# One decoder step in fp32: the order of items, dense groups and outputs in the attention ticks

## The reference

```
h  = RMSNorm(x) * (1 + a1) + s1                       # a1, s1, ... = silu(c) @ w_ada + b_ada
[q | k | v | hc | B | C | ga | gb] = h @ w_in
A-branch: stick-breaking attention, 8 heads x 64, strictly causal
          A[t,s] = beta[t,s] * prod_{s<j<t} (1 - beta[t,j]),  beta = sigmoid(q.k/8 + b)
B-branch: y = B * dwconv3_causal(C * hc)
mix = (sigmoid(ga) * (o_att @ w_att_out) + sigmoid(gb) * (y @ w_conv_out)) @ w_o
x   = x + g1 * mix
x   = x + g2 * sqrelu_mlp(RMSNorm(x) * (1 + a2) + s2)
```

## Time and profile before

| | us |
|---|---|
| median of 3 runs | 1631.52 (1631.40 to 1632.21) |
| profiled execution, its own time | 1631.7 |
| its span, first to last instruction | 1629.9 |
| v product ends, ticks begin | about 188 |
| last tick's scores (tick 47) begin | 701.3 |

### The profile page before, as it was taken

How to read it: one execution, slowest core, us unless ns; L and a number is a source line. 1 busy time by engine, 2 the same in 40 slices (tenths; PEclk the granted TensorE clock), 3 DMA queues, 4 the chain that set the end, 5 groups by cost and what they waited for, 6 DMA issues and landing times.

```text
span 1629.9 us, 31959 instructions
## 1 busy us (share of the span) xinstructions
PE 1614.5 (99%) x12386; PEld 1509.1 (93%) x12386; DVE 901.1 (55%) x1631; ACT 463.3 (28%) x813; POOL 607.4 (37%) x424
## 2 busy tenths in 40 slices
PE   9999999999999999999999999999999999999999
PEld 7998788888888888899999999999999999999999
DVE  5654354554544344335532699566666666666666
ACT  5444222222222223233222453222222222222220
POOL 0245043343334334322121127444444444444440
PEclk9999999999999999999999999999999999999999
DMA  9113347666656676434421111111111111111112
GB/s 383 51 47 97 140 149 234 226 214 224 200 190 220 216 244 229 169 132 173 163 103 50 40 39 44 49 52 44 37 52 52 52 53 53 52 53 52 52 40 107
DMA packets 72230, 194.76 MB, mean 119 GB/s; under 512 B 8049, under 2 KB 8562, under 8 KB 72082
## 3 DMA queue, kind: packets, MB, share of 16 engines
q1 hardware_dynamic: 67682, 178.62, 32.5%
q10 hardware_dynamic: 4400, 14.10, 2.3%
HBM read 174.26 MB, written 18.42 MB: 118 GB/s over the span
## 4 chain that ended last, share of the span: by engine, by line
PE 93%; DVE 2%; DMA 1%; ACT 1%; POOL 1%; issue 1%; SPq 0%; ACTq 0%; POOLq 0%; DVEq 0%
PE psum L820 78%; PE psum L961 2%; PE psum L984 2%; PE psum L1008 2%; PE psum L972 2%; PE psum L1033 2%; PE psum L852 1%; DMA ring<-in_cache_v 1%; POOL wl L721 1%; DVE h2L L1865 1%; DVE sc L1897 1%; PE psum L881 1%; DMA xt<-in_xT 0%; PE psum L883 0%; PE psum L882 0%
## 5 line engine op out<-in xcount | busy, mean ns | idle before, releaser
L803 POOL TENSOR_TENSOR wl<-raw,wh 128x512 fp32r<-128x512 f32 x148 | 212.8, 1443 | 317.0 <-ACT wh L1441 316.9
L820 PE MATMUL psum<-hH,wh 128*128 128x352 f32 x808 | 269.1, 333 | 0.1
L820 PE MATMUL psum<-hL,wh 128*128 128x352 f32 x808 | 260.0, 322 | 0.0
L820 PE MATMUL psum<-hH,wl 128*128 128x352 f32 x808 | 259.3, 321 | 0.0
L820 PE MATMUL psum<-hidH,wh 128*128 128x352 f32 x768 | 247.4, 322 | 0.0
L820 PE MATMUL psum<-hidH,wl 128*128 128x352 f32 x768 | 247.2, 322 | 0.0
L820 PE MATMUL psum<-hidL,wh 128*128 128x352 f32 x768 | 247.1, 322 | 0.0
L746 POOL TENSOR_TENSOR beta<-beta,kb 128x512 f32<-128x512 f32 (+3 forms) x96 | 122.5, 1297 | 251.2 <-DVE kb L1661 251.2
L721 POOL TENSOR_TENSOR wl<-raw,wh 128x1024 fp32r<-128x1024 f32 x49 | 119.7, 2442 | 231.5 <-ACT wh L1306 231.0
L820 PEld LDWEIGHTS psum<-hH,wh 128*128 128x128 f32 x808 | 151.6, 188 | 30.3 <-issue 29.3
L1984 DVE SCALAR_TENSOR_TENSOR act<-psum,mods,act 128x352 f32<-128x352 f32 x256 | 145.4, 579 | 50.5 <-PE psum L820 50.5
(11 more groups left out here) (255 smaller groups left out, 3257.3 us busy)
## 6 DMA issues: line engine op xcount, KB each, us to landing
raw<-in_weights SPq DMA_DIRECT2D x152, 512.0 KB, 3.7
ring<-in_cache_k SPq DMA_DIRECT2D x128, 256.0 KB, 4.0
ring<-in_cache_v SPq DMA_DIRECT2D x128, 256.0 KB, 3.7
pre<-in_weights SPq DMA_DIRECT2D x16, 512.0 KB, 16.6
gate_scratch<-gt ACTq DMA_DIRECT2D x14, 528.0 KB, 3.6
act<-gate_scratch SPq DMA_DIRECT2D x14, 528.0 KB, 4.6
xt<-in_xT SPq DMA_DIRECT2D x8, 528.0 KB, 6.9
act<-in_xT SPq DMA_DIRECT2D x8, 528.0 KB, 4.9
```

What stands on the lines that cost most here:

```text
L803: pool.tensor_tensor(xl, source_of(i), x.bitcast(F32), ALU.subtract).then_inc(S["split"], 1)
L820: mm = pe.matmul(out, x, y, start=n == 0, stop=n == end)
```

## The change

Five edits.

1. **Schedule.** Items stand in each of the ticks 0 to 33 (before: in three of four ticks, up to tick 44). The `single` ticks are now k % 12 in (3, 5, 7, 9, 10, 11), and 1 and 13, all below 34; after tick 33 each tick has two dense groups. Ticks with an item are thus 34 in a row, 18 of them with one dense group. What stands in the ticks that matter:

| tick (n of the step) | before: A, B | after: A, B | after: item scores, `ada`, `ada` turn |
|---|---|---|---|
| 9 (384) | B17.1, - | C16.2, - | 9, yes, no |
| 10 (256) | B17.2, - | B17.0 (late), - | 10, yes, yes |
| 20 (512) | B23.0 (late), B23.1 | hc21.2, C22.0 | 20, yes, yes |
| 22 (256) | gate24.0, - | C22.2, - | 22, yes, yes |
| 23 (128) | gate24.1, gate24.2 | B23.0 (late), - | 23, yes, yes |

(C16.2 is the third group of unit 16, of kind C.)

2. **First tick.** In tick 0 TensorE does group A ahead of the waits and scores, and group B straight after the scores.
3. **Outputs.** ScalarE's table load and the output DMAs of k and of the prompt's v move into the v product's loop; that of the sample's v goes to the end of tick 0.
4. **VectorE's preparation** of `qb` no longer waits for the v product's end.
5. **History copy.** The copy of the conv history into `us` moves from the first `C` group's eviction to just ahead of the item's scan (one tick later where that group is a `DENSE_B`).

```diff
-    single = [k for k in range(NSTEP) if k % 12 in (1, 5, 9, 10) or k in (16, 40)]
+    single = [k for k in range(NITEM) if k % 12 in (3, 5, 7, 9, 10, 11) or k in (1, 13)]
...
-        if k % 4 != 3 and m < NITEM:
+        if m < NITEM:
...
+HISTORY_AT = {}
+for _at, _more in ((DENSE_A, 0), (DENSE_B, 1)):
+    for _k, _g in _at.items():
+        if GROUPS[_g].kind == "C" and GROUPS[_g].c == 0:
+            HISTORY_AT[_k + _more] = (GROUPS[_g].u - 12) // 3
...
-            pe.wait_ge(S["qk_ready"], QK_N)
-            pe.wait_ge(S["bank_dve"], evictions("mix", "d"))
-            pe.wait_ge(S["bank_act"], evictions("mix", "a"))
-
...
             for k in range(TICKS):
-                if k < NSTEP:
+                if k == 0:
+
+                    dense(DENSE_A[k], hH, hL)
+                    pe.wait_ge(S["qk_ready"], QK_N)
+                    pe.wait_ge(S["bank_dve"], evictions("mix", "d"))
+                    pe.wait_ge(S["bank_act"], evictions("mix", "a"))
                     scores(k)
-                if k in DENSE_A:
+                    dense(DENSE_B[k], hH, hL)
+                elif k < NSTEP:
+                    scores(k)
+                if k in DENSE_A and k:
                     dense(DENSE_A[k], hH, hL)
...
-                if k in DENSE_B:
+                if k in DENSE_B and k:
                     dense(DENSE_B[k], hH, hL)
...
-            act.preload_act_table_set("sigmoid_and_others")
-            act.wait_ge(S["qk_ready"], QK_N)
-            for p in range(NPAIR):
-                act.dma_start(a["kT"][:, p, :], act8[:, NPAIR + p, :]).then_inc(S["kout"], 16)
-            act.wait_ge(S["bank_act"], 9)
-            act.dma_start(a["v"][0:SEQ].rearrange("(t p) c -> p t c", p=P), vsb[:, 0:8, :]).then_inc(S["vout"], 16)
-            act.dma_start(a["v"][SEQ:T], vsb[0:NS, 8, :]).then_inc(S["vout"], 16)
+                if t == 5:
+                    act.preload_act_table_set("sigmoid_and_others")
+                if t == 6:
+                    act.wait_ge(S["qk_ready"], QK_N)
+                    for p in range(NPAIR):
+                        act.dma_start(a["kT"][:, p, :], act8[:, NPAIR + p, :]).then_inc(S["kout"], 16)
+                if t == 7:
+                    act.wait_ge(S["bank_act"], 8)
+                    act.dma_start(a["v"][0:SEQ].rearrange("(t p) c -> p t c", p=P), vsb[:, 0:8, :]).then_inc(S["vout"], 16)
...
+                if k == 0:
+                    act.wait_ge(S["bank_act"], 9)
+                    act.dma_start(a["v"][SEQ:T], vsb[0:NS, 8, :]).then_inc(S["vout"], 16)
...
-            dve.wait_ge(S["dense_done"], MIX0)
             mark(dve.memset(qb[:, :, :], 0.0))
-            mark(dve.memset(up[:, SEQ:SEQ + 2], 0.0))
-            for s in range(4):
-                mark(dve.memset(beta[s][:, 0:1], 0.0))
...
+            dve.wait_ge(S["dense_done"], MIX0)
+            mark(dve.memset(up[:, SEQ:SEQ + 2], 0.0))
...
-                    if c == 0:
-                        mark(cp(us[:, :, 4:6], sm("hist", 16 * cb, 16 * cb + 16).rearrange("p (b j) -> p b j", j=2)))
...
+                if k in HISTORY_AT:
+                    history(HISTORY_AT[k])
                 if k in ITEM_AT:
                     sample_scan(ITEM_AT[k])
```

More of the change, by code:

```diff
@@ L318 @@
 ticks()
+HISTORY_AT = {}
[3 more added lines that the diff above has]
+            HISTORY_AT[_k + _more] = (GROUPS[_g].u - 12) // 3
+assert len(HISTORY_AT) == CB
 SLOTS = ("scores", "dense_a", "sturn", "turn", "sscore", "dense_b", "ada", "sav", "av")
@@ L1630, in _ @@
             dve.wait_ge(S["qk_ready"], QK_N)
-            dve.wait_ge(S["dense_done"], MIX0)
             mark(dve.memset(qb[:, :, :], 0.0))
-            mark(dve.memset(up[:, SEQ:SEQ + 2], 0.0))
-            for s in range(4):
-                mark(dve.memset(beta[s][:, 0:1], 0.0))
-            for s in (0, 1):
-                mark(dve.memset(sbeta[s][:, 0:1], 0.0))
             own()
@@ L1645, in _ @@
                         one.then_inc(S["qb_ready"], 1)
+            dve.wait_ge(S["dense_done"], MIX0)
+            mark(dve.memset(up[:, SEQ:SEQ + 2], 0.0))
+            for s in range(4):
+                mark(dve.memset(beta[s][:, 0:1], 0.0))
+            for s in (0, 1):
+                mark(dve.memset(sbeta[s][:, 0:1], 0.0))
+            own()
             def keep_and_scan(k):
@@ L1758, in evict, with history @@
                         dve.sem_inc(S["yc_ready"], 1)
+            def history(cb):
+                mark(cp(us[:, :, 4:6], sm("hist", 16 * cb, 16 * cb + 16).rearrange("p (b j) -> p b j", j=2)))
             def split_lo(c):
```

## The result

| | before | after |
|---|---|---|
| median | 1631.46 us (4 runs) | 1642.04 us (4 runs, 1639.80 to 1643.12) |
| ratio after to before | | 1.0062, 95% interval 1.0050 to 1.0074 |
| profiled execution | 1631.7 | 1639.8 (span 1638.0) |

The change costs 8.1 us in the profiled execution and 10.6 by the medians. Slower by more than 0.2% was forecast at 0.70, with 1637.4 as the time, in a range of 1630.5 to 1645; the forecast's own range, without its rivals, was 1634 to 1642.

What follows compares the result with a forecast made beforehand. TensorE, busy 99%, bounds the kernel, so only waits change: 2.6 + 6.2 + 2.0 - 4.9 = +5.9 on 1631.7 profiled, which is 0.2 over the median: 1637.4 us. Range 1634 to 1642, with rivals 1630.5 to 1645.

Steps and rivals of the forecast that it cites:

- first tick: From the v product to tick 1, TensorE's 11.8 us span shrinks: 1.8 us gained (bounds 1.0 and 2.3).
- tick 2's history copy: In tick 2, the copy moved ahead of the item's scan ends TensorE's wait: 0.8 us gained.
- old V waits, tick 21, `ada` block: Waits of 1.3, 0.7 and 0.3 us fall on ticks made up anew: 2.3 us gained if nothing replaces them.
- `ada` turns, others: Ten turns wait 4.3 us for VectorE's weights copy behind group A's eviction: 2.6 us more (bounds 0 and 4).
- ticks 10 and 23: `ada` copy behind convolution and late V overlap, the longer wait counts: 6.2 us for both ticks (bounds 5 and 10).
- other V pages: V late in other ticks with one group B between: 2.0 us more (0 to 9.6).
- the items named with a spill: Ticks 26 to 32, where ScalarE spills a gate at the same moment: four such ticks carry the 2.0 us.
- The sum without this term: By the 358 GB/s HBM rule no other V comes late, while the 6.2 us stays: 1635.4 us.
- half of two rivals: Wider range 1630.5 to 1645 us: half of the not-slower rival and the lower half of the load rival.
- Loads do not set the pace: Rival: in the ticks with items, loads set the pace and every blocked V takes 15.2 us; +17.7, 1649.2 us; chance 0.10.
- The first tick's gain was real: Rival: the first tick gains nothing, another wait replaces the output DMAs; +1.8, 1639.2 us; chance 0.06.
- Not slower: Rival: VectorE and SP are in time in ticks 10 and 23; -0.3, 1631.2 us; chance 0.24.

Runs made afterwards that it cites:

- V first: Changed kernel with an item's V load ahead of the raw load on SP's queue in the same tick: 1639.45 us, ratio 1.0050.
- the run with both: Changed kernel with V loads ahead of raw loads and VectorE's `ada` copy ahead of the convolution: 1629.90 us, ratio 0.9989.
- new schedule alone: Kernel before with only the changed schedule; first tick, outputs, VectorE's preparation and history copy as before: 1647.72 us, ratio 1.0100.
- `ada` copy first: Changed kernel with VectorE's `ada` copy ahead of the convolution where group A opens a B unit: 1643.41 us, ratio 1.0075.
- all orders, old schedule: Changed kernel, schedule of the kernel before; V ahead of raw loads, `ada` copy ahead of convolution, transposed-weights copy ahead of group A's eviction: 1627.37 us.
- all orders, new schedule: Changed kernel with V ahead of raw loads, `ada` copy ahead of convolution, transposed-weights copy ahead of group A's eviction: 1626.02 us, ratio 0.9967.

## Why the prediction was right, point by point

| term | forecast | measured (profiled execution) |
|---|---|---|
| first tick | -1.8 | -2.0 |
| tick 2's history copy | -0.8 | -0.8 |
| old V waits, tick 21, `ada` block | -2.3 | -2.3 |
| `ada` turns, others | +2.6 (4.3 in all, ten) | +2.0 (3.6, nine) |
| ticks 10 and 23 | +6.2 | +5.8 of waits |
| other V pages | +2.0 | +3.4 (five waits, 0.4 to 1.4) |
| clock behind the wait of tick 10 | none | +1.7 |
| sum | +5.9 | +7.8 |

The sum of the measured terms is 0.3 short of the 8.1 by which the profiled execution is longer.

- **What bounds it, and the method.** Right: TensorE's busy time stayed (1614.5 us before, 1615.0 after, the slower matmuls of tick 10 included), and the waits account for most of the difference. Most of the rest is the clock, below.
- **Ticks 10 and 23.** Both mechanisms were there and lay over each other: V's wait of 2.2 and 3.6 (forecast 2.4 and 3.0), and under it, once V was early, the `ada` copy at 2.97 and 2.46 (forecast 3.0 to 3.1). The runs with one edit and with both show it. In tick 23 V's wait came out 0.6 longer than forecast, the copy's 0.5 shorter.
- **Other V pages.** Mis-sized: 3.4 instead of 2.0. The prediction names these pages by the tick of their item's scores; each wait stands at the end of the tick after. Four of the five were of the items named with a spill (26, 28, 30, 32; 0.6, 1.4, 0.6, 0.4), the fifth of item 12 (0.4), where nothing was taken. V ahead of the raw loads removed all five; that the spill adds to them is not shown. The prediction's list leaves out items 1, 16 and 18, which also have a raw load ahead and one group B between; they did not wait. The sum without this term, 1635.4, in which no other V comes late, did not hold.
- **`ada` turns.** Right in cause, and 0.7 too large in all; moving the copy ahead of the eviction took them from 4.7 to 2.1.
- **The missing term: the clock.** The forecast took the full clock for granted, from the ticks of before. The lower level behind a wait cost 1.7 us in the profiled execution. Not all of it is extra: the `ada` copy of tick 10 ended only at 308.07, and at the full clock the second head's scores would have waited for it some 0.6 us (an estimate: in the run with V first TensorE came to them 2.26 after the item's values began, and went on 0.25 after the copy). So the longer of the two waits did count in tick 10, as forecast, and about 1.1 of the clock's 1.7 came on top. The other three of the changed kernel have mean clocks of 0.997 and 0.998 instead of 0.999, 1.6 us for each 0.001, which is about as much as they are longer (2.2 to 3.3 us); where their clock fell no trace shows. So the median lies 4.6 us above the forecast: inside the range of 1630.5 to 1645, which allows for half of two rivals, and at the very edge of the forecast's own (1642.04, against 1642). The mechanism was right; the size was low by the clock and by the other V pages.
- **The rivals.** Loads do not set the pace: with the same loads in another order no V wait was left. The first tick's gain was real: 2.0 in the trace, and 2.7 with the other parts in the old schedule. "Not slower" would have needed both orders mended: the run with both gave 1629.9, and neither edit alone did.

## What to carry to other kernels

When items are packed closer, look for waits that the old spacing hid, at each place of the plan where an in-order queue holds something urgent behind something that is not ready: here V pages behind a raw load, and a 0.3 us copy behind some 4 us of convolution and eviction. Two such waits at one place hide each other, so a fix of one shows little there (5.8 us of V waits became 5.4 of the copy's); the term is the longer of the two, and both must be mended before the schedule pays. An idle stretch of TensorE can also have a price after it, in matmuls at the lower clock: 1.7 us each time here.

## What the runs showed that was not expected

In the profiled executions the granted clock fell to 1.2 GHz for some 3.5 us, 1.7 us lost each time, behind these waits of TensorE: 1.48, 3.22 and 2.89 us (new schedule alone, ticks 8, 10 and 23), 1.70 (both edits, tick 24), 2.19 (changed kernel, tick 10), 2.97 and 2.46 (V loads first, ticks 10 and 23) and 2.73 (`ada` copy first, tick 10). It did not fall behind 3.57 (changed kernel, tick 23), 2.85 (`ada` copy first, tick 23), 1.98 (all orders, old schedule), 1.48 (kernel before, first tick), 1.39 (changed kernel, tick 29) and 1.30 (all orders, new schedule). So the length of the wait alone does not tell it, and the mean clock of the same program differs from execution to execution. What decides was not tried.
